# Moved steps in the attention queues, and compressed scores written 64 columns wide, in a hybrid SSD and sparse-attention block

## The chip, the cores and the metric

The kernel runs on one core of one Trainium2 chip. The metric is the device time of one execution in microseconds (us); less is better. A core has five queues that run side by side and meet only at semaphores: PE (TensorE, the matrix engine), DVE (VectorE), ACT (ScalarE), POOL (GpSimd) and SP (SyncE, which here issues the loads). Each queue works strictly in the order in which the kernel writes it down.

## The reference, cut to what matters

One layer takes a 512x1024 float32 input through a norm, a wide projection, a chunked state-space branch, an attention branch, a gated mix of both and an MLP. The change lies in the attention branch. It has 16 heads of 64 columns in 4 key groups, and three kinds of attention: over 31 compressed keys, over selected blocks and over a window. At 512 tokens the selection takes every block and the window covers every earlier token, so the last two are plain causal attention with different keys and values:

```python
s_c = jnp.einsum('bqgrd,bkgd->bgrqk', qn, kc).astype(jnp.float32) * scale
p_c = masked_softmax(s_c, cmp_end[None, :] <= t[:, None])
o_c = jnp.einsum('bgrqk,bkgd->bqgrd', p_c.astype(vc.dtype), vc)
...
s_s = jnp.einsum('bqgrd,bgqkd->bgrqk', qr, k_sel).astype(jnp.float32) * scale
p_s = masked_softmax(s_s, m_s)
o_s = jnp.einsum('bgrqk,bgqkd->bqgrd', p_s.astype(v_sel.dtype), v_sel)
...
o = gate[:, :, 0] * o_c + gate[:, :, 1] * o_s + gate[:, :, 2] * o_w
```

`qn` is the query before the rotary step, `qr` the one after it. `o_w` is made as `o_s`, with the window's keys and values.

## The kernel before, in words

The whole layer is one hand-scheduled program. Every large product is made in three parts to reach float32 accuracy: each operand is split into a high part (`whi`, `h_hi`, `q_hl`, `o_hi`) and the rest (`wlo`, `h_lo`, `o_lo`). A **unit** is one product of a 1024x128 block of weights with all 512 tokens: SP loads `raw`, ACT writes `whi` from it, POOL writes `wlo` (the function `low`, L834), PE multiplies. Two slots alternate.

Eight units make the queries (`q_unit`). After each, ACT writes a plain scaled copy `q_s` (`q_plain`), DVE makes the two products of the rotary step (`cos_q`), a small DMA swaps rows, DVE adds them (`rope_q`, L1520), ACT writes the high part (`high_q`) and DVE the low part (`low_q`, two halves of 64 rows, L1527). `cmp_scores(rr, pp)` multiplies `q_s` with the compressed keys `kc`: eight matmuls of 128 tokens each, whose results stand 64 columns apart in one bank. Seven of them are 128 columns wide, and the next one writes over the right half of what it left; only 64 columns of each are read, by `cmp_read` on DVE.

The attention itself is a loop over 64 **pairs** n. `pair(n)` gives the half of the heads rr (32 pairs each), the block of 128 tokens i (from 3 down to 0), the key group g, and br (0 selected, 1 window). A pair is two heads (r2), `width(n)` = 128 (i+1) keys wide: 512 for n 0 to 7, 384 for 8 to 15, then 256 and 128; the last two are `narrow`. The steps of a pair go round the engines:

- PE `scores(n)` (L2209, mask L2213), ahead of use by two pairs, or more for narrow ones (the table `ahead`)
- DVE `row_max(n)` (L1581, L1584; narrow L1578)
- ACT `exp(n, r2)` (L1005), which also sums the row
- DVE `over_sum(n)` (L1592), one over the sums
- POOL multiplies the probabilities with that and the gate (L854)
- PE `turn(n)` (L2248) transposes them, four 128x128 blocks a head at i=3, into one of two banks; before it takes a bank again it waits for the copy out of it two turns ago (`turn_to`, the list `copied`)
- ACT and DVE `copy_turned(n)` (L1041, L1606), one head each
- PE `weigh(n)` (L2269) multiplies with the values; for an odd n a matmul of the compressed part follows (L2277)
- ACT `high_out(a)` (L1012) and DVE `low_out(a)` (L1612) write the output of the two pairs 2a, 2a+1

The compressed part goes a block at a time: `cmp_centre`, `cmp_exp`, `cmp_probs`, `cmp_gates`, then PE `turn_cmp(c)` (L2236) and ACT `copy_cmp(c)` (L1022, writes `pcT`). `turn_cmp(0)` shares the two turn banks: it stands between the turns of pair 0 and pair 1, so it needs ACT's copy of pair 0, and the second head of `turn(1)` needs `copy_cmp(0)`.

The order around the change is written out by hand, one loop over n for each engine. Three things are in those loops that don't belong to the pairs: POOL's last two `low` (for the first two units of the state-space part, which PE reaches only after the attention), and the end of the query work for units 6 and 7, which the pairs from n=32 on use.

Of the kernel before, what the change touches and what calls it, by code (L numbers as in the profile page):

```python
# [28 lines left out]
P = 128  # L29
S = 512  # L30
# [35 lines left out]
U_SSM = U_Q + 8  # L66
# [69 lines left out]
def build(nc, a, out):  # L136

    ctx = ExitStack()
    with ctx:
# [364 lines left out]
        def narrow(n):  # L504
            return width(n) <= 256
# [319 lines left out]
        def _(pool):  # L825
# [18 lines left out]
            pool.wait_ge(whi_ready, U_SSM + 1)  # L844
            low(0)

            for n in range(PAIRS):
                rr, i, g, br = pair(n)
                pool.wait_ge(over_sum_ready, n + 1)
                for r2 in range(2):  # L850
                    at_step = 2 * n + r2
                    column = 16 * (br + 1) + g * R + 2 * rr + r2
                    rows = prob_rows(n, r2)
                    nc.gpsimd.tensor_scalar(rows, rows, rsum[:, at_step % 16:at_step % 16 + 1], gate[:, i, column:column + 1],  # L854
                                            ALU.mult, ALU.mult).then_inc(prob_ready, 1)
                if n == 2:
                    pool.wait_ge(whi_ready, U_SSM + 2)
                    low(1)
# [12 lines left out]
        def _(act):  # L871
# [181 lines left out]
            for n in range(PAIRS):  # L1053
                long = [m for m in ahead[n + 1] if not narrow(m)]
                if long:
                    exp(long[0], 0)
                if n == cmp_pair(0):
                    copy_cmp(0)
# [5 lines left out]
                for m in long[1:]:  # L1064
                    exp(m, 0)
                    exp(m, 1)
                for m in ahead[n + 1]:
                    if narrow(m):
                        exp(m, 0)
                        exp(m, 1)  # L1070
                if n % 8 == 2 and n < 58:
                    cmp_exp(n // 8 + 1)
                if n % 2 == 1 and n >= 3:
                    high_out((n - 3) // 2)
                if n in (2, 4):
                    high_q(5 + n // 2)
# [231 lines left out]
        def _(dve):  # L1308
# [213 lines left out]
            def low_q(u):  # L1522

                for e in range(2):
                    rows = slice(e * HD, (e + 1) * HD)
# [110 lines left out]
            low_q(5)  # L1636
            cos_q(7)
            for n in range(PAIRS):
                for m in ahead[n + 1]:
                    row_max(m)  # L1640
                for m in sums_at[n + 1]:
                    over_sum(m)
# [3 lines left out]
                if n < 2:  # L1646
                    rope_q(6 + n)
                if n == 2:
                    cmp_read(1, 1)
                if n in (3, 5):  # L1650
                    low_q(6 + n // 4)
# [381 lines left out]
        def _(pe):  # L2033
# [146 lines left out]
            def cmp_scores(rr, pp):  # L2180
# [7 lines left out]
                for i in range(NC):  # L2188
                    for r2 in range(2):
                        n = (i * 2 + r2) * 64  # L2190
                        w = min(P, S - n)
# [400 lines left out]
```

## Time and profile before

| | |
|---|---|
| median of 3 runs | 1281.34 us (1280.8 to 1281.37) |
| the profiled execution | 1279.05 us |
| its span in the trace | 1277.1 us |
| PE busy | 1247.4 us, 98% of the span |
| DVE, ACT, POOL busy | 763.3, 584.4, 404.0 us |
| granted TensorE clock | 0.998 of full speed |
| query units and attention | about 110 to 330 us |

The span is what lies between the first and the last instruction. A timeline row gives the start of a group of like instructions, how long they lasted together, the engine, the line, what is written and read, the shape, how many (xN), and in brackets the idle time of the engine before them and what ended it. A float32 matmul shows up as two records (two passes), each with its own weight load on the row PEld. Matmul records overlap each other, so a group's time holds the pipeline's depth once.

### The profile page before, as it was taken

The page shows a single profiled execution, that of the slowest core. Times are in us where ns is not written, and L with a number is a line of the kernel's source. Part 1 is how long each engine was busy: PE and PEld are TensorE (multiplying, and loading weights), DVE is VectorE, ACT ScalarE, POOL GpSimd, SP SyncE. Part 2 cuts the span into 40 slices and gives each one's busy share as a digit, 9 for nine tenths or more (in the row PEclk, how much of TensorE's full clock was granted, in tenths as well). Part 3 has the DMA queues.
Part 4 walks back from the last instruction along what each step waited for, and adds up shares of the span by engine and source line. Part 5 has one row for each costly group of instructions (what it writes and reads, how often), then busy time and mean ns, then how long its engine had stood idle before and what let it go on. Part 6 is the DMA issues. An engine that isn't in the chain of part 4 may idle for free.

```text
span 1277.1 us, 19195 instructions
## 1 busy us (share of the span) xinstructions
PE 1247.4 (98%) x6742; PEld 1026.5 (80%) x6742; DVE 763.3 (60%) x1353; ACT 584.4 (46%) x1016; POOL 404.0 (32%) x270
## 2 busy tenths in 40 slices
PE   8999989999999999999999999999999999999997
PEld 7887866777788888888888888888878888888885
DVE  6845876676477777877784111111147849479487
ACT  6325466666444544454453222222356446254364
POOL 3432344545332333333333444444430110201200
PEclk9999999999999999999999999999999999999999
DMA  8523410000123222322222333333443061340501
GB/s 242 157 70 71 93 37 2 2 2 2 50 66 83 68 80 66 82 66 72 76 70 79 98 91 93 97 99 108 172 161 119 17 214 33 112 151 16 201 12 66
DMA packets 172312, 108.40 MB, mean 85 GB/s; under 512 B 25220, under 2 KB 163814, under 8 KB 172262
## 3 DMA queue, kind: packets, MB, share of 16 engines
q1 hardware_dynamic: 172022, 107.65, 28.8%
q8 instruction: 30, 0.49, 0.2%
q14 instruction: 20, 0.16, 0.0%
q10 hardware_dynamic: 240, 0.09, 0.0%
HBM read 104.84 MB, written 2.10 MB: 84 GB/s over the span
## 4 chain that ended last, share of the span: by engine, by line
PE 86%; ACT 4%; DVE 4%; issue 2%; POOL 1%; DMA 1%; SPq 1%; DVEq 0%; ACTq 0%; POOLq 0%
PE bank L2424 20%; PE bank L2046 17%; PE bank L2433 10%; PE bank L2050 9%; PE bank L2528 8%; PE bank L2533 4%; PE bank L2443 2%; PE bank L2269 2%; PE bank L2209 2%; PE bank L2248 2%; ACT prob L1005 1%; POOL prob L854 1%; PE bank L2106 1%; PE bank L2449 1%; PE bank L2404 1%
## 5 line engine op out<-in xcount | busy, mean ns | idle before, releaser
L834 POOL TENSOR_TENSOR wlo<-raw,whi 128x1024 fp32r<-128x1024 f32 x133 | 325.1, 2445 | 717.7 <-ACT whi L1083 388.6
L1083 ACT ACTIVATE whi<-raw 128x1024 fp32r<-128x1024 f32 x96 | 101.8, 1060 | 295.7 <-PE bank L2433 160.0
L2046 PE MATMUL bank<-h_hi,whi 128*128 128x512 f32 x488 | 194.4, 398 | 0.7 <-DVE h_lo L1327 0.7
L2046 PE MATMUL bank<-h_lo,whi 128*128 128x512 f32 x488 | 190.4, 390 | 0.0
L2424 PE MATMUL bank<-h_hi,whi 128*128 128x512 f32 x384 | 150.3, 391 | 1.3 <-DVE grp L1766 0.7
L2424 PE MATMUL bank<-h_lo,whi 128*128 128x512 f32 x384 | 149.5, 389 | 0.0
L2050 PE MATMUL bank<-h_hi,wlo 128*128 128x512 f32 x488 | 120.8, 390 | 0.0
L2046 PEld LDWEIGHTS bank<-h_hi,whi 128*128 128x128 f32 x488 | 91.8, 188 | 21.1 <-DVE h_lo L1327 2.5
L1854 DVE TENSOR_TENSOR mt<-bank,sig 128x512 f32<-128x512 f32 x16 | 11.1, 691 | 161.6 <-PE bank L2433 161.6
L1746 DVE SCALAR_TENSOR_TENSOR grp<-bank,vt,grp 128x511 f32<-128x511 f32 (+2 forms) x96 | 71.8, 748 | 59.0 <-ACT grp L1107 50.1
L2050 PEld LDWEIGHTS bank<-h_hi,wlo 128*128 128x128 f32 x488 | 91.6, 188 | 19.1
L2046 PEld LDWEIGHTS bank<-h_lo,whi 128*128 128x128 f32 x488 | 91.8, 188 | 17.6
L854 POOL TENSOR_SCALAR prob<-prob,rsum,gate 128x512 f32<-128x512 f32 (+3 forms) x128 | 77.4, 619 | 79.2 <-DVE rsum L1592 79.1
L2433 PE MATMUL bank<-h_hi,wlo 128*128 128x512 f32 x384 | 94.8, 389 | 0.0
L2424 PEld LDWEIGHTS bank<-h_hi,whi 128*128 128x128 f32 x384 | 72.1, 188 | 18.5 <-DVE h_lo L1894 2.7
L1005 ACT ACTIVATE prob<-bank,nmax 128x512 f32<-128x512 f32 (+3 forms) x128 | 66.7, 531 | 44.0 <-DVE nmax L1581 38.5
L2433 PEld LDWEIGHTS bank<-h_hi,wlo 128*128 128x128 f32 x384 | 72.1, 188 | 15.0
L2424 PEld LDWEIGHTS bank<-h_lo,whi 128*128 128x128 f32 x384 | 72.1, 188 | 14.6
L1235 ACT ACTIVATE whi<-raw 128x1024 fp32r<-128x1024 f32 x30 | 31.7, 1057 | 79.2 <-PE bank L2433 60.9
L2248 PE MATMUL bank<-cst,prob 128*128 128x128 f32 x320 | 49.0, 278 | 12.6 <-POOL prob L854 9.5
L1917 DVE TENSOR_TENSOR comb<-comb 128x256 f32<-128x256 f32 x64 | 30.2, 492 | 49.5 <-ACT comb L1273 49.0
L1967 DVE TENSOR_TENSOR x<-bank,x 128x512 f32<-128x512 f32 x64 | 41.1, 683 | 21.3 <-PE bank L2533 21.3
(318 smaller groups left out, 2501.3 us busy)
## 6 DMA issues: line engine op xcount, KB each, us to landing
raw<-in_w_in SPq DMA_DIRECT2D x75, 512.0 KB, 3.8
raw<-in_w_up SPq DMA_DIRECT2D x32, 512.0 KB, 4.1
draw<-in_w_down SPq DMA_DIRECT2D x16, 1024.0 KB, 6.6
raw<-in_w_ssm_branch SPq DMA_DIRECT2D x16, 512.0 KB, 3.6
raw<-in_w_in SPq DMA_DIRECT2D x20, 256.0 KB, 3.8
raw<-in_w_attn_branch SPq DMA_DIRECT2D x8, 512.0 KB, 3.6
raw<-in_w_o SPq DMA_DIRECT2D x8, 512.0 KB, 3.7
x_sb<-in_x SPq DMA_DIRECT2D x4, 512.0 KB, 5.1
```

The source lines that it names most:

```text
L834: nc.gpsimd.tensor_tensor(wlo[slot][:], raw[slot][:], whi[slot][:].bitcast(F32), ALU.subtract).then_inc(wlo_ready, units)
L854: nc.gpsimd.tensor_scalar(rows, rows, rsum[:, at_step % 16:at_step % 16 + 1], gate[:, i, column:column + 1], ALU.mult, ALU.mult).then_inc( ...
L1005: nc.scalar.activation(prob_rows(n, r2), bank[b][:, off:off + width(n)], ACT.Exp, bias=nmax[:, at_step % 16:at_step % 16 + 1], accum_out=e ...
L1083: nc.scalar.activation(whi[slot][:], raw[slot][:], ACT.Copy).then_inc(whi_ready, 1)
L1746: ins = V.scalar_tensor_tensor(grp[:, j, back:S], bank[j % 2][:, 0:S - back], vt[:, bass.ds(tile + (V_CW + (CONV - 1 - back) * 32), 1)], g ...
L2046: T.matmul(bank[slot][:], whi[slot][:, k * P:(k + 1) * P], part[:, k, :], start=(k == 0 and n == 0), stop=False)
L2050: mm = T.matmul(bank[slot][:], wlo[slot][:, k * P:(k + 1) * P], h_hi[:, k, :], start=False, stop=(k == KT - 1))
L2248: mm = T.transpose(to[:, off + t * P:off + (t + 1) * P], prob_rows(n, r2)[:, t * P:(t + 1) * P], ident)
L2424: T.matmul(to[:], whi[slot][:, k * P:(k + 1) * P], part[:, k0 + k, :], start=(start and k == 0 and n == 0), stop=False)
L2433: mm = T.matmul(to[:], wlo[slot][:, k * P:(k + 1) * P], hi[:, k0 + k, :], start=False, stop=(stop and k == KT - 1))
L2528: T.matmul(bank[at_bank + t][:], part[:, 2 * (n % 2) + kl, which, t * P:(t + 1) * P], half_slot(n, 0)[:, kl, :], start=(fresh and n % 2 == ...
L2533: return T.matmul(bank[at_bank + t][:], comb_hi[:, 2 * (n % 2) + kl, which, t * P:(t + 1) * P], half_slot(n, 1)[:, kl, :], start=False, st ...
```

## The change

Six edits, all in the attention part:

1. POOL: the two `low` calls stood before the loop and after pair 2; now they stand after pair 1 and after pair 3.
2. ACT: at n=1 `copy_cmp(0)` goes ahead of the first exp of that round.
3. ACT: `high_out` goes ahead of the exps of narrow pairs. That moves it at n=13 and n=45 alone.
4. ACT and DVE: `high_q(7)` goes from n=4 to n=6, `rope_q(7)` from n=1 to n=4. `low_q(6)` went whole at n=3 and goes in halves at n=6 and 7; `low_q(7)` went whole at n=5 and goes in halves at n=8 and 10.
5. DVE: `over_sum(1)` goes from the loop's first round to a place ahead of `cos_q(7)`.
6. PE: all eight matmuls of `cmp_scores` are 64 columns wide.

```diff
--- before.py
+++ after.py
@@ -841,9 +841,6 @@
                 for slot in range(2):
                     pool.wait_ge(whi_ready, two * 2 + (slot + 1))
                     low(slot)
-            pool.wait_ge(whi_ready, U_SSM + 1)
-            low(0)
-
             for n in range(PAIRS):
                 rr, i, g, br = pair(n)
                 pool.wait_ge(over_sum_ready, n + 1)
@@ -853,9 +850,9 @@
                     rows = prob_rows(n, r2)
                     nc.gpsimd.tensor_scalar(rows, rows, rsum[:, at_step % 16:at_step % 16 + 1], gate[:, i, column:column + 1],
                                             ALU.mult, ALU.mult).then_inc(prob_ready, 1)
-                if n == 2:
-                    pool.wait_ge(whi_ready, U_SSM + 2)
-                    low(1)
+                if n in (1, 3):
+                    pool.wait_ge(whi_ready, U_SSM + n // 2 + 1)
+                    low(n // 2)
 
             with pool.Fori(U_SSM // 2 + 1, U_MLP // 2) as two:
                 for slot in range(2):
@@ -1052,10 +1049,10 @@
             q_split(7)
             for n in range(PAIRS):
                 long = [m for m in ahead[n + 1] if not narrow(m)]
+                if n == cmp_pair(0):
+                    copy_cmp(0)
                 if long:
                     exp(long[0], 0)
-                if n == cmp_pair(0):
-                    copy_cmp(0)
                 copy_turned(n)
                 if n and n % 8 == 0:
                     copy_cmp(n // 8)
@@ -1064,16 +1061,16 @@
                 for m in long[1:]:
                     exp(m, 0)
                     exp(m, 1)
+                if n % 2 == 1 and n >= 3:
+                    high_out((n - 3) // 2)
                 for m in ahead[n + 1]:
                     if narrow(m):
                         exp(m, 0)
                         exp(m, 1)
                 if n % 8 == 2 and n < 58:
                     cmp_exp(n // 8 + 1)
-                if n % 2 == 1 and n >= 3:
-                    high_out((n - 3) // 2)
-                if n in (2, 4):
-                    high_q(5 + n // 2)
+                if n in (2, 6):
+                    high_q(6 + n // 4)
             high_out(PAIRS // 2 - 1)
 
             def split_next(landed, done, slot):
@@ -1519,9 +1516,11 @@
                 roped = vtmp[:, u % 2, :]
                 V.tensor_tensor(roped, roped, rope_to[u % 2][:], ALU.add).then_inc(q_ready, 1)
 
-            def low_q(u):
+            def low_q(u, only=None):
 
                 for e in range(2):
+                    if only not in (None, e):
+                        continue
                     rows = slice(e * HD, (e + 1) * HD)
                     dve.wait_ge(qhi_ready, 2 * u + e + 1)
                     V.tensor_tensor(q_hl[(1 - e) * HD:(2 - e) * HD, 2 * u + e, :], vtmp[rows, u % 2, :],
@@ -1634,21 +1633,23 @@
             cmp_gates(0)
             cmp_read(1, 0)
             low_q(5)
+            over_sum(1)
             cos_q(7)
             for n in range(PAIRS):
                 for m in ahead[n + 1]:
                     row_max(m)
                 for m in sums_at[n + 1]:
-                    over_sum(m)
+                    if m >= 2:
+                        over_sum(m)
                 copy_turned(n)
                 if n % 2 == 1 and n >= 3:
                     low_out((n - 3) // 2)
-                if n < 2:
-                    rope_q(6 + n)
+                if n in (0, 4):
+                    rope_q(6 + n // 4)
                 if n == 2:
                     cmp_read(1, 1)
-                if n in (3, 5):
-                    low_q(6 + n // 4)
+                if n in (6, 7, 8, 10):
+                    low_q(6 + n // 8, (0, 1, 0, 1)[(6, 7, 8, 10).index(n)])
                 if n % 8 == 1 and n < 57:
                     cmp_centre(n // 8 + 1)
                 if n % 8 == 3 and n < 59:
@@ -2188,7 +2189,7 @@
                 for i in range(NC):
                     for r2 in range(2):
                         n = (i * 2 + r2) * 64
-                        w = min(P, S - n)
+                        w = 64
                         mm = T.matmul(to[:, n:n + w], q_s[:, 2 * pp + r2, i * P:(i + 1) * P],
                                       kc[:, pp, 0:w], start=True, stop=True)
                 mm.then_inc(cs_ready, 1)
```

Nothing is added and nothing taken out; SP's queue is as it was. Below are three places where it moves instructions. Line numbers of the changed kernel are up to three lower (L854 becomes L851, L1005 L1002, L1012 L1009, L1527 L1526).

**POOL, from the end of the loop over query units into the pairs.** `prob0` and `prob1` hold pair 0, `prob2` and `prob3` pair 1, `prob4` and `prob5` pair 2. Before:

```order
L834 TENSOR_TENSOR wlo0_68<-raw0_64,whi0_66 128x1024
L854 ISA
L854 TENSOR_SCALAR prob0_115<-prob0_115,rsum_110,gate_57 128x512
L854 TENSOR_SCALAR prob1_116<-prob1_116,rsum_110,gate_57 128x512
L854 TENSOR_SCALAR prob2_117<-prob2_117,rsum_110,gate_57 128x512
L854 TENSOR_SCALAR prob3_118<-prob3_118,rsum_110,gate_57 128x512
L854 TENSOR_SCALAR prob4_112<-prob4_112,rsum_110,gate_57 128x512
L854 TENSOR_SCALAR prob5_122<-prob5_122,rsum_110,gate_57 128x512
L834 TENSOR_TENSOR wlo1_69<-raw1_65,whi1_67 128x1024
L854 TENSOR_SCALAR prob0_115<-prob0_115,rsum_110,gate_57 128x512
```

Now:

```order
L851 TENSOR_SCALAR prob0_115<-prob0_115,rsum_110,gate_57 128x512
L851 TENSOR_SCALAR prob1_116<-prob1_116,rsum_110,gate_57 128x512
L851 TENSOR_SCALAR prob2_117<-prob2_117,rsum_110,gate_57 128x512
L851 TENSOR_SCALAR prob3_118<-prob3_118,rsum_110,gate_57 128x512
L834 TENSOR_TENSOR wlo0_68<-raw0_64,whi0_66 128x1024
L851 TENSOR_SCALAR prob4_112<-prob4_112,rsum_110,gate_57 128x512
L851 TENSOR_SCALAR prob5_122<-prob5_122,rsum_110,gate_57 128x512
L851 TENSOR_SCALAR prob0_115<-prob0_115,rsum_110,gate_57 128x512
L851 TENSOR_SCALAR prob1_116<-prob1_116,rsum_110,gate_57 128x512
L834 TENSOR_TENSOR wlo1_69<-raw1_65,whi1_67 128x1024
```

Both `wlo` rows moved down: the first from ahead of pair 0 to behind pair 1, the second from behind pair 2 to behind pair 3.

**ACT, in the round n=13.** `prob1` is the second head of pair 15, the rows with x2 are pairs 16 and 17, `o_hi` is `high_out(5)`, the `pT0` row behind is the copy of pair 14. Before:

```order
L1041 ACTIVATE pT0_128<-bank5 128x384
L1005 ACTIVATE prob1_116,esum_109<-bank1,nmax_108 128x384
L1005 ACTIVATE prob2_117,esum_109<-bank2,nmax_108 128x256 x2
L1005 ACTIVATE prob3_118,esum_109<-bank3,nmax_108 128x256 x2
L1012 ACTIVATE o_hi_72<-bank7 128x128
L1041 ACTIVATE pT0_128<-bank5 128x384
```

Now:

```order
L1038 ACTIVATE pT0_128<-bank5 128x384
L1002 ACTIVATE prob1_116,esum_109<-bank1,nmax_108 128x384
L1009 ACTIVATE o_hi_72<-bank7 128x128
L1002 ACTIVATE prob2_117,esum_109<-bank2,nmax_108 128x256 x2
L1002 ACTIVATE prob3_118,esum_109<-bank3,nmax_108 128x256 x2
L1038 ACTIVATE pT0_128<-bank5 128x384
```

`high_out(5)` moved up past the four exps of two narrow pairs. The same happens at n=45.

**DVE, in the rounds n=3 and n=4.** The first `pT0` row is the copy of pair 3, `o_lo` is `low_out(0)`, the three rows on `cst8` and `cs` are `cmp_probs(1)`, and `nmax` from bank2 and bank3 is `row_max(6)`. Before:

```order
L1592 RECIPROCAL rsum_110<-esum_109 128x2
L1606 COPY pT0_128<-bank4 128x512
L1612 TENSOR_TENSOR o_lo_73<-bank6,o_hi_72 128x128
L1527 TENSOR_TENSOR q_hl_119<-vtmp_96,q_hl_119 64x512 x2
L1555 TENSOR_REDUCE cst8_111<-cs_121 128x8
L1557 TENSOR_TENSOR cs_121<-cs_121,cst_49 128x2x128
L1559 RECIPROCAL cst8_111<-cst8_111 128x8
L1581 TENSOR_REDUCE nmax_108<-bank2 128x1
L1584 TENSOR_REDUCE nmax_108<-bank3 128x1
```

Now:

```order
L1591 RECIPROCAL rsum_110<-esum_109 128x2
L1605 COPY pT0_128<-bank4 128x512
L1611 TENSOR_TENSOR o_lo_73<-bank6,o_hi_72 128x128
L1554 TENSOR_REDUCE cst8_111<-cs_121 128x8
L1556 TENSOR_TENSOR cs_121<-cs_121,cst_49 128x2x128
L1558 RECIPROCAL cst8_111<-cst8_111 128x8
L1580 TENSOR_REDUCE nmax_108<-bank2 128x1
L1583 TENSOR_REDUCE nmax_108<-bank3 128x1
```

The two halves of `low_q(6)` are gone from between `low_out(0)` and `row_max(6)`. The same holds for `low_q(7)` two rounds on.

## Rows read from the trace of the kernel before

**Rows 1.** The page: PE's busy time (share of the span), and the chain by engine.

```profile
PE 1247.4 (98%) x6742; PEld 1026.5 (80%) x6742; DVE 763.3 (60%) x1353; ACT 584.4 (46%) x1016; POOL 404.0 (32%) x270
...
PE 86%; ACT 4%; DVE 4%; issue 2%; POOL 1%; DMA 1%; SPq 1%; DVEq 0%; ACTq 0%; POOLq 0%
```

**Rows 2.** Waits of PE over the whole span: total, times, longest in us.

```profile
PE bank L2248 <- POOL prob L854: 9.5, 8, 3.0
...
PE bank L2248 <- ACT pcT L1022: 1.4, 1, 1.4
```

**Rows 3.** Timeline of PE, 163 to 196 us: start, duration, work, [idle before].

```profile
166.35 1.41 PE L2248 MATMUL bank<-cst,prob 128*128 128x128 f32 x8 [2.96 <-POOL prob L854]
...
167.51 0.70 PE L2209 MATMUL bank<-kw,q_hl 128*128 128x512 f32 x2
...
168.71 0.39 PE L2236 MATMUL bank<-cst,cs 128*128 128x128 f32 x2
...
170.93 0.63 PE L2248 MATMUL bank<-cst,prob 128*128 128x128 f32 x4 [1.39 <-ACT pcT L1022]
...
173.75 1.04 PE L2248 MATMUL bank<-cst,prob 128*128 128x128 f32 x8
...
186.76 1.41 PE L2248 MATMUL bank<-cst,prob 128*128 128x128 f32 x8 [0.92 <-POOL prob L854]
...
194.77 1.41 PE L2248 MATMUL bank<-cst,prob 128*128 128x128 f32 x8 [1.27 <-POOL prob L854]
```

**Rows 4.** Timeline of POOL, 162 to 175 us.

```profile
162.80 2.67 POOL L834 TENSOR_TENSOR wlo<-raw,whi 128x1024 fp32r<-128x1024 f32 x1 [11.76 <-ACT whi L977]
165.53 3.03 POOL L854 TENSOR_SCALAR prob<-prob,rsum,gate 128x512 f32<-128x512 f32 x4
...
171.95 2.38 POOL L834 TENSOR_TENSOR wlo<-raw,whi 128x1024 fp32r<-128x1024 f32 x1
```

**Rows 5.** Timeline of ACT, 165 to 171 us.

```profile
165.19 0.69 ACT L1005 ACTIVATE prob<-bank,nmax 128x512 f32<-128x512 f32 x1 [1.05 <-DVE nmax L1581]
...
167.04 0.60 ACT L1041 ACTIVATE pT<-bank 128x512 f32<-128x512 f32 x1 [1.07 <-PE bank L2248]
...
170.41 0.37 ACT L1022 ACTIVATE pcT<-bank 128x256 f32<-128x256 f32 x1
```

**Rows 6.** Timeline of DVE, 155 to 184 us.

```profile
155.71 0.17 DVE L1592 RECIPROCAL rsum<-esum 128x2 f32<-128x2 f32 x1 [0.70 <-ACT prob L1005]
...
172.20 2.67 DVE L1520 TENSOR_TENSOR vtmp<-vtmp,rope_to 128x512 f32<-128x512 f32 x1
...
182.18 1.40 DVE L1527 TENSOR_TENSOR q_hl<-vtmp,q_hl 64x512 fp32r<-64x512 f32 x2
```

**Rows 7.** Timeline of PE, turns of pairs 13 and 15, 213 to 221 us.

```profile
213.35 0.82 PE L2248 MATMUL bank<-cst,prob 128*128 128x128 f32 x6
...
219.87 1.20 PE L2248 MATMUL bank<-cst,prob 128*128 128x128 f32 x6 [1.62 <-POOL prob L854]
```

**Rows 8.** Timeline of PE, turn of pair 47, 298 us.

```profile
298.49 1.19 PE L2248 MATMUL bank<-cst,prob 128*128 128x128 f32 x6 [1.63 <-POOL prob L854]
```

**Rows 9.** Timeline of ACT, round n=13, 214 to 217 us.

```profile
214.82 0.48 ACT L1005 ACTIVATE prob<-bank,nmax 128x256 f32<-128x256 f32 x1
...
216.62 0.31 ACT L1012 ACTIVATE o_hi<-bank 128x128 fp32r<-128x128 f32 x1
```

**Rows 10.** Timeline of DVE, `low_out(5)` in round n=13.

```profile
216.96 0.29 DVE L1612 TENSOR_TENSOR o_lo<-bank,o_hi 128x128 fp32r<-128x128 f32 x1 [2.19 <-ACT o_hi L1012]
```

**Rows 11.** Timeline of PEld, wide passes of the first `cmp_scores`.

```profile
127.37 0.75 PEld L2192 LDWEIGHTS bank<-kc,q_s 128*128 128x128 f32 x6
```

**Rows 12.** Timeline of PEld, last two wide and both 64-column passes, next unit's load.

```profile
128.27 0.53 PEld L2192 LDWEIGHTS bank<-kc,q_s 128*128 128x128 f32 x4
128.71 0.19 PEld L2175 LDWEIGHTS bank<-h_hi,whi 128*128 128x128 f32 x1
```

**Rows 13.** Timeline of PE, eight 512-column matmuls of a query unit.

```profile
151.86 1.98 PE L2175 MATMUL bank<-h_hi,wlo 128*128 128x512 f32 x8
```

## The prediction

> **What bounds the kernel now.** The page comes first: PE is busy 98% of the span, and 86% of the chain that ended last is PE's [rows 1]. So time is won only where PE stands still or does less. The waits of PE come second: its one large item is `turn` waiting for POOL's multiplied probabilities, 9.5 us in 8 places, and one of 1.4 us for ACT's `pcT` [rows 2]. The timeline of PE comes third, to see where these lie: 2.96 us before `turn(0)`, 1.39 before the second head of `turn(1)`, 0.92 before `turn(5)`, 1.27 before `turn(7)` [rows 3], 1.62 before `turn(15)` [rows 7], and 1.63 at the same place of the second half, `turn(47)` [rows 8]. They sum to 9.8 us. The reader should see that each has another releaser behind the one named: POOL is a relay, and what made it late is found on POOL, ACT and DVE.
>
> A turn that had to wait also runs slower, since its second head's probabilities come while the first is being turned: 1.41 us for eight records against 1.04 for one that never waited [rows 3], 1.20 for six against 0.82 [rows 7], 1.19 for pair 47 [rows 8]. That is 0.37 us more at each of the last four places. At `turn(0)` I count nothing more, since POOL was then working through both pairs anyway.
>
> **The change part by part.**
>
> *POOL's first `low`, and `over_sum(1)`.* The sums of pair 0 were inverted on DVE at 155.71 [rows 6], but POOL first did `wlo` from 162.80 to 165.47 and only then pair 0 at 165.53 [rows 4]. Now pair 0 is ready before PE wants it: the 2.96 us go. What is late next is ACT. PE's wait began at 166.35 - 2.96 = 163.39. From there it does `turn(0)` in about 1.0 us and `scores(3)` in 1.2 (167.51 to 168.71), and at about 165.6 comes to `turn_cmp(0)`, which needs ACT's copy of pair 0. ACT does that behind the first exp of pair 2, begun at 165.19 [rows 5]; with `over_sum(1)` now ahead on DVE I take 165.3. Exp 0.69 and copy 0.60 give 166.6: a new wait of 1.0 us.
>
> *`copy_cmp(0)` ahead of an exp.* Before, `pcT` was written at 170.41, behind an exp [rows 5] whose row maximum came late; PE got on at 170.93. Now it stands right behind the second exp of pair 2: 166.6 + 0.69 + 0.37 = 167.6, while PE, with 0.2 for `turn_cmp` and 0.44 for four transposes, is there at 167.3. The wait of 1.39 becomes 0.3. Left of both: 1.3 us. `over_sum(1)` itself is 0.17 us on DVE and gives POOL pair 1 early, so that `wlo` (2.4 us) fits in ahead of pair 2.
>
> *Where `wlo` now falls.* `rope_q(7)` took 2.67 us when it ran beside the second `wlo`, ending 0.5 us after it [rows 4, 6]; its like take 0.7. Now `rope_q(6)` falls beside the first `wlo` (about 165.0 to 167.4) and should end near 167.9. Pair 2 is then multiplied from about 169.1, its first head done at 169.9; PE turns it at about 170.4. Hidden, with half a microsecond in hand. The two `wlo` blocks themselves end at most 2 us later than before. The loads of SP that wait for them, and PE's use of them, belong to the part behind the attention, some 150 us on: nothing.
>
> *`low_q` out of rounds 3 and 5.* `low_q(6)` held DVE for 1.40 us at 182.18 [rows 6], ahead of `row_max(6)` and `over_sum(5)`, and `turn(5)` waited 0.92 for that; `low_q(7)` did the same to `turn(7)`, 1.27. Taking 1.4 us out of the way is more than either. Gone: 0.92 + 0.37 and 1.27 + 0.37, 2.9 us. The work comes back: 0.7 us of `rope_q(7)` in round 4, 0.7 in each of rounds 6, 7, 8 and 10, and 1.3 on ACT in round 6. Walking the queues with the durations of their rows, I find probabilities ready some 0.4 us before PE wants them in rounds 7 to 13, so a bare 0.7 us mostly fits. But in even rounds the piece stands right behind `over_sum`, when POOL starts on two multiplications of 0.76 us each (3.03 for four [rows 4]), and it reads two tiles of SBUF as `rope_q(7)` did. Waiting one of them out is 0.76, or 0.36 over the margin; for three such pieces about 0.9 us is paid back (bounds: 0, and three times 0.76, 2.3).
>
> By the Trainium skill (SBUF — State Buffer, "Who interferes with whom") a tensor_tensor with both inputs in SBUF contends with GpSimd's reads, and whichever starts first blocks the other for its whole instruction. The 2.67 us beside `wlo` agree. By that rule every piece beside a multiplication pays, and the payback is nearer its upper bound.
>
> *`high_out` ahead of narrow exps.* In round 13 ACT went through four exps of pairs 16 and 17, from 214.82 to 216.62, before `high_out(5)` [rows 9]. DVE stood 2.19 us for it [rows 10], and behind `low_out(5)` lay `over_sum(15)`, for which `turn(15)` waited. DVE gets on 1.8 us sooner; the wait was 1.62. Gone: 1.62 + 0.38, and 1.63 + 0.37 at `turn(47)`, 4.0 us. The exps start 0.3 us later; DVE inverts their sums only behind two more row maxima.
>
> *64 columns in place of 128.* 28 matmuls, 56 passes. Six weight loads of wide passes start within 0.75 - 0.19 = 0.56 us, 0.112 apart [rows 11]. The last four, two of them for 64-column passes, start within 0.53 - 0.19 = 0.34, 0.113 apart, and the next unit's load follows at 128.71, no sooner [rows 12]. A narrow pass takes as long as a wide one, because its 128 columns of weights do. Bounds: 0, and 3.1 us (56 times half of 0.112) if the pass shrank with its columns. I take 0, the row that is the thing itself.
>
> By the Trainium skill (TensorE: Matmul & The Clock Gate, "Step-by-step: what each phase is for") a matmul's throughput is purely its N moving columns. By that rule 64 columns fewer at 2.4 GHz would save an estimated 27 ns a pass, 1.5 us in all. In this trace a 512-column matmul costs 0.227 us, (1.98 - 0.39) / 7 [rows 13], so streaming does set the pace there, at 0.44 ns a column.
>
> **The sum.** Removed: 2.96 + 1.39 + 1.29 + 1.64 + 2.00 + 2.00 = 11.3 us. Left at the start 1.3, paid back 0.9. Gain 9.1 us. From the profiled execution's 1279.05 that is 1269.9; from the median, which lies 2.3 higher, 1281.34 - 9.1 = **1272.2 us**.
>
> **The rivals.**
>
> *The ring of DVE and ACT takes over.* DVE waits for `o_hi`, ACT for the row maximum, so one round feeds the next. With PE's early stalls gone, the 2.8 us of DVE work moved into rounds 6 to 10 comes where the margin is thin, and the waits at `turn(5)`, `turn(7)` and `turn(15)` come back at other turns. For: DVE had the same work in all. Against: its 2.19 us of idle time in round 13. It keeps 11.3 - 1.3 - 4.9 = 5.1 us: 1276.2.
>
> *The narrow writes count.* The forecast less 1.6 us (56 passes by 64 columns by 0.44 ns [rows 13]) to 3.1: 1270.6 to 1269.1. Against: the loads' pace [rows 12].
>
> *Waits only move.* `turn_cmp(0)` stands as long as `turn(0)` did, ACT being slower through `high_q(5)` and the last splits than I think, and the later stalls shift. About 1280.
>
> *Slower.* Place: rounds 6 to 10. Price: four halves of `low_q` at 0.7, each waiting 0.76 for POOL, and `high_q(7)` at 1.3 ahead of an exp: 7.1 us on a ring that is then the bound, with only `turn(47)`'s 2.0 kept: 1286.4. It decides once DVE has no idle time left in rounds 8 to 13. The 2.19 us [rows 10] speak against it.
>
> **How the numbers follow.** Forecast 0.62 (its own range 1270.3 to 1274.5), ring 0.20, narrow writes 0.08, waits only move 0.06, slower 0.04. A difference of 0.2%, 2.6 us, is about what a measurement can tell from none. Three cases are faster by more: 0.90; same 0.06, slower 0.04. The range takes in the first three, 1269.0 to 1277.0.
>
> **What would show it.** The waits of PE for POOL fall from 9.5 us to under 3. `turn(15)` and `turn(47)` wait for nothing, and DVE's 2.19 us before `o_lo` are gone. In round 1 a wait of about 1 us for ACT's copy stands before `turn_cmp(0)`. Weight loads of `cmp_scores` are still 0.112 us apart. It is wrong if new waits of PE for POOL stand in rounds 7 to 13 (then the ring), if the loads come closer together (then the narrow writes), or if PE waits some 3 us before `turn_cmp(0)`.

## The result: 1271.6 us, and the profile after

The changed kernel takes **1271.59 us** (median of 4 runs, 1270.12 to 1272.79), the kernel before 1281.07 beside it (4 runs). The ratio is 0.9927, 95% interval 0.991 to 0.9944: 7.2 to 11.5 us less. 1272.2 was forecast.

The page of the changed kernel, answering to [rows 1]:

```profile
PE 1249.4 (98%) x6742; PEld 1030.6 (81%) x6742; DVE 762.2 (60%) x1353; ACT 583.8 (46%) x1016; POOL 405.3 (32%) x270
...
PE 87%; DVE 4%; ACT 3%; issue 2%; POOL 1%; DMA 1%; SPq 1%; DVEq 0%; ACTq 0%; POOLq 0%
```

PE is as busy as before in a shorter span, and still carries the chain. The waits of PE (line waited for: total, times, longest), answering to [rows 2]:

```profile
PE bank L2249 <- POOL prob L851: 1.4, 4, 0.4
...
PE bank L2237 <- ACT pT L1038: 1.3, 1, 1.3
```

For POOL it waits 1.4 us in place of 9.5, and no wait for `pcT` is long enough to be listed. New is one of 1.3 before `turn_cmp(0)` (L2237). PE's timeline has the places of [rows 3, 7, 8]; `turn` is now L2249:

```profile
168.43 0.41 PE L2237 MATMUL bank<-cst,cs 128*128 128x128 f32 x2 [1.32 <-ACT pT L1038]
168.69 1.34 PE L2249 MATMUL bank<-cst,prob 128*128 128x128 f32 x8
...
202.95 0.55 PE L2249 MATMUL bank<-cst,prob 128*128 128x128 f32 x3 [0.27 <-POOL prob L851]
...
214.20 1.20 PE L2249 MATMUL bank<-cst,prob 128*128 128x128 f32 x6
...
291.18 1.19 PE L2249 MATMUL bank<-cst,prob 128*128 128x128 f32 x6
```

In order these are `turn_cmp(0)`, `turn(1)`, the second head of `turn(11)`, `turn(15)` and `turn(47)`. The last two have no wait that is listed (PE is idle 0.03 us before each), but take 1.20 and 1.19 us, as long as before.

**The start.** ACT and POOL at the same place, answering to [rows 4, 5]:

```profile
167.02 0.69 ACT L1002 ACTIVATE prob<-bank,nmax 128x512 f32<-128x512 f32 x1 [1.11 <-DVE nmax L1580]
...
167.70 0.59 ACT L1038 ACTIVATE pT<-bank 128x512 f32<-128x512 f32 x1
...
168.87 0.38 ACT L1019 ACTIVATE pcT<-bank 128x256 f32<-128x256 f32 x1
```

```profile
165.30 1.52 POOL L851 TENSOR_SCALAR prob<-prob,rsum,gate 128x512 f32<-128x512 f32 x2 [6.04 <-DVE rsum L1591]
166.78 2.35 POOL L834 TENSOR_TENSOR wlo<-raw,whi 128x1024 fp32r<-128x1024 f32 x1
```

POOL now does pair 0 first. ACT copies pair 0 behind the exp that began at 167.02, and `turn_cmp(0)` follows that copy. The copy of `pcT` ends at 169.25, while PE is in `turn(1)`, and the second head of that turn starts right behind it:

```profile
169.40 0.30 PE L2249 MATMUL bank<-cst,prob 128*128 128x128 f32 x1
```

That is late as well: the turn takes 1.34 us for eight records, 1.04 where nothing is late. It is too short a gap (0.08 us of idle time) to be listed as a wait.

**Rounds 4 to 13.** DVE, with `rope_q(6)` and `rope_q(7)` (L1517), the four halves of `low_q` (L1526) and `low_out(5)` (L1611), answering to [rows 6, 10]:

```profile
168.10 1.58 DVE L1517 TENSOR_TENSOR vtmp<-vtmp,rope_to 128x512 f32<-128x512 f32 x1
...
183.17 0.90 DVE L1517 TENSOR_TENSOR vtmp<-vtmp,rope_to 128x512 f32<-128x512 f32 x1
...
189.32 0.79 DVE L1526 TENSOR_TENSOR q_hl<-vtmp,q_hl 64x512 fp32r<-64x512 f32 x1
...
193.35 0.69 DVE L1526 TENSOR_TENSOR q_hl<-vtmp,q_hl 64x512 fp32r<-64x512 f32 x1
...
195.65 0.81 DVE L1526 TENSOR_TENSOR q_hl<-vtmp,q_hl 64x512 fp32r<-64x512 f32 x1
...
201.54 0.81 DVE L1526 TENSOR_TENSOR q_hl<-vtmp,q_hl 64x512 fp32r<-64x512 f32 x1
...
211.06 0.29 DVE L1611 TENSOR_TENSOR o_lo<-bank,o_hi 128x128 fp32r<-128x128 f32 x1 [0.36 <-ACT o_hi L1009]
```

The wait before `low_out(5)` is 0.36 us; it was 2.19. POOL's multiplications in these rounds:

```profile
185.48 1.53 POOL L851 TENSOR_SCALAR prob<-prob,rsum,gate 128x512 f32<-128x512 f32 x2 [0.76 <-DVE rsum L1591]
188.81 1.95 POOL L851 TENSOR_SCALAR prob<-prob,rsum,gate 128x512 f32<-128x512 f32 x2 [1.80 <-DVE rsum L1591]
191.56 1.30 POOL L851 TENSOR_SCALAR prob<-prob,rsum,gate 128x384 f32<-128x384 f32 x2 [0.81 <-DVE rsum L1591]
195.26 1.73 POOL L851 TENSOR_SCALAR prob<-prob,rsum,gate 128x384 f32<-128x384 f32 x2 [2.39 <-DVE rsum L1591]
...
201.16 1.74 POOL L851 TENSOR_SCALAR prob<-prob,rsum,gate 128x384 f32<-128x384 f32 x2 [2.08 <-DVE rsum L1591]
```

A pair that a piece of `low_q` fell beside took 1.95 us in place of 1.53, or 1.73 in place of 1.30. The piece beside it took 0.79 to 0.81, and 0.69 where it fell beside none (193.35). The two heads of the pair at 188.81, one by one:

```profile
188.81 0.77 POOL L851 TENSOR_SCALAR prob<-prob,rsum,gate 128x512 f32<-128x512 f32 x1 [1.80 <-DVE rsum L1591]
...
189.55 1.20 POOL L851 TENSOR_SCALAR prob<-prob,rsum,gate 128x512 f32<-128x512 f32 x1
```

The first took its usual 0.77; the piece (189.32 to 190.11) began only 0.25 us before that ended; the second took 1.20, so all of POOL's 0.43 lies there.

**Where the 9.1 us lie.** From the first query unit's first matmul to the last matmul of the attention, the changed kernel takes 207.75 us, the kernel before 216.84: 9.09 us less. I call this the **stretch** from here on. Behind it the two traces keep their distance. The profiled executions themselves lie only 6.3 us apart (1272.79 and 1279.05): this one lost 1.7 us ahead of the stretch, where the program is the same, and 1.0 us more of its time lies outside the trace's span (1272.79 less 1269.8, against 1279.05 less 1277.1). The first 17 us of the changed kernel, then of the one before (busy time, PE's with records, granted clock, DMA share, GB/s):

```profile
0.00:17.00 17.00, 14.09 (x85) 0.90 0.81 231
```

```profile
0.00:17.00 17.00, 13.71 (x90) 1.00 0.84 233
```

The clock there was 0.90 against 1.00. So I compare stretches. Each is that of one execution.

The sum can be checked inside the stretch: for each pair, its turn's start is counted from the first query unit's matmul in both traces, and the difference is what has been gained so far.

| up to | forecast, this part | measured, this part | gained so far |
|---|---|---|---|
| turn(3) | 3.05 (4.35 removed, 1.3 left) | 2.99 | 2.99 |
| turn(6) | 1.29 | 1.44 | 4.43 |
| turn(8) | 1.64 | 1.79 | 6.22 |
| turn(14) | -0.9 | -0.42 | 5.80 |
| turn(15) | 2.00 | 1.59 | 7.39 |
| turn(47) | 2.00 | 1.60, and 0.05 between | 9.04 |

### The profile page after: what moved, and what is told of

Same layout as the page of the kernel before. It is cut to its first block, busy times and chain, and to the rows that moved or that the text cites. A ratio compares the mean times of both kernels' runs of the same rounds, so it can differ in the third digit from the quotient of the medians.

```text
span 1269.8 us, 19195 instructions
## 1 busy us (share of the span) xinstructions
PE 1249.4 (98%) x6742; PEld 1030.6 (81%) x6742; DVE 762.2 (60%) x1353; ACT 583.8 (46%) x1016; POOL 405.3 (32%) x270
## 4 chain that ended last, share of the span: by engine, by line
PE 87%; DVE 4%; ACT 3%; issue 2%; POOL 1%; DMA 1%; SPq 1%; DVEq 0%; ACTq 0%; POOLq 0%
PE bank L2425 21%; PE bank L2047 17%; PE bank L2434 10%; PE bank L2051 8%; PE bank L2529 8%; PE bank L2534 4%; PE bank L2270 2%; PE bank L2444 2%; PE bank L2210 2%; PE bank L2249 2%; POOL prob L851 1%; PE bank L2107 1%; PE bank L2450 1%; PE bank L2405 1%; ACT prob L1002 1%
## 5 line engine op out<-in xcount | busy, mean ns | idle before, releaser
L851 POOL TENSOR_SCALAR prob<-prob,rsum,gate 128x512 f32<-128x512 f32 (+3 forms) x128 | 78.9, 629 | 80.7 <-DVE rsum L1591 80.7
L1002 ACT ACTIVATE prob<-bank,nmax 128x512 f32<-128x512 f32 (+3 forms) x128 | 66.7, 534 | 37.0 <-DVE nmax L1580 33.8
L2249 PE MATMUL bank<-cst,prob 128*128 128x128 f32 x320 | 48.6, 278 | 2.9 <-POOL prob L851 1.4
```

What stands on the lines that cost most here:

```text
L1002: nc.scalar.activation(prob_rows(n, r2), bank[b][:, off:off + width(n)], ACT.Exp, bias=nmax[:, at_step % 16:at_step % 16 + 1], accum_out=e ...
L2249: mm = T.transpose(to[:, off + t * P:off + (t + 1) * P], prob_rows(n, r2)[:, t * P:(t + 1) * P], ident)
```

## The experiments

The theory: the gain comes from PE's six waits, each ended by work moved out of an engine's queue; the narrow writes do nothing. Its rivals: the narrow writes carry part of it; or edits only pay in company. Four kernels are the kernel before with one part of the change alone. (Edits 2 and 5 were not run alone.) Each ratio below is to the kernel before as timed in the same session (medians 1280.02, 1281.16 and 1280.81 us), with its 95% interval; it can differ from the quotient of the medians by 0.1%.

**Narrow writes alone.**

```diff
-                        w = min(P, S - n)
+                        w = 64
```

> The kernel before, with the 64-column writes alone. The attention stretch (first query-unit matmul to the last attention matmul) was 216.84 us before and 207.75 with the whole change. Theory (a pass is paced by the load of its 128 weight columns): the loads stay 0.112 us apart, the stretch stays at 216.8 within 0.1, the time within 0.1% of before. Rival (a pass costs its moving columns): 56 passes shorter by 0.028 to 0.056, so the stretch is 215.3 to 213.7.

Measured: 1280.77 us, ratio 1.0007 (0.9997 to 1.0017), stretch 216.91 against 216.84. `turn(0)`, behind three of the four blocks, starts 0.01 us earlier than before. They are worth nothing.

**`high_out` alone.**

```diff
+                if n % 2 == 1 and n >= 3:
+                    high_out((n - 3) // 2)
                 for m in ahead[n + 1]:
                     if narrow(m):
```

> The kernel before, with high_out ahead of the narrow exps alone. Theory (ACT's four exps of 1.8 us stand before high_out(5), DVE's low_out(5) and the sums of pair 15): the waits of 1.62 and 1.63 before turn(15) and turn(47) go to 0.1, the second head of each turn still comes late, the stretch is 216.84 - 3.2 = 213.6, the time 3.2 us less. Rival (POOL, or the row maxima of pairs 18 and 19 ahead of the sums, hold turn(15)): waits of 1 us and more stay, gain under 1.5.

Measured: 1276.02 us, ratio 0.9967 (0.9954 to 0.9979), stretch 213.87: 2.97 less. Counted up to each turn, 1.59 come at `turn(15)` and 1.6 at `turn(47)`; 0.17 was lost at the start, on which more below.

**POOL's `low` and `over_sum(1)` alone.**

```diff
-            pool.wait_ge(whi_ready, U_SSM + 1)
-            low(0)
...
-                if n == 2:
+                if n in (1, 3):
...
+            over_sum(1)
             cos_q(7)
```

> The kernel before, with POOL's low and over_sum(1) moved alone. Theory (the wait of 2.96 is replaced by one for ACT's copy, and pcT is still behind an exp whose row maximum is late): PE waits about 1.3 before turn_cmp(0) and about 1.1 for pcT, gain 1.5 to 2.0 of the 4.35 that both first waits cost. Rival (the whole 2.96 goes, since pair 0 is all that PE lacked): gain 3 or more.

Measured: 1281.01 us, ratio 1.0008 (0.9998 to 1.0017), and the stretch 1.4 us **longer**, 218.28. That is a miss. PE's timeline of this kernel:

```profile
166.62 0.41 PE L2235 MATMUL bank<-cst,cs 128*128 128x128 f32 x2 [1.40 <-ACT pT L1038]
166.86 0.60 PE L2247 MATMUL bank<-cst,prob 128*128 128x128 f32 x4
169.71 1.08 PE L2247 MATMUL bank<-cst,prob 128*128 128x128 f32 x4 [2.24 <-ACT pcT L1019]
170.72 1.98 PE L2268 MATMUL bank<-pT,vtok 128*64 128x128 f32 x16
172.63 1.22 PE L2208 MATMUL bank<-ks,q_hl 128*128 128x512 f32 x2
```

The 2.96 us are gone, but 1.40 and 2.24 took their place, and what follows is slow: `weigh` (L2268) took 1.98 us for sixteen records that take 1.09 elsewhere. The granted clock says why:

```profile
168.00:170.00 2.00, 0.29 (x2) 0.76 0.61 164
170.00:172.00 2.00, 2.00 (x16) 0.50 0.36 107
...
174.00:176.00 2.00, 2.00 (x9) 0.53 0.00 0
```

From about 169.0, in the second wait, to 175.9 PE's clock was at 0.50, its level of 1.2 GHz. The wait of 2.24 is for `pcT`, which ACT writes behind an exp whose row maximum stands on DVE behind `rope_q(6)`, itself slowed by `wlo`:

```profile
166.28 1.59 DVE L1517 TENSOR_TENSOR vtmp<-vtmp,rope_to 128x512 f32<-128x512 f32 x1
167.80 0.68 DVE L1578 TENSOR_REDUCE nmax<-bank 128x1 f32<-128x512 f32 x1
```

```profile
168.51 0.69 ACT L1002 ACTIVATE prob<-bank,nmax 128x512 f32<-128x512 f32 x1 [1.37 <-DVE nmax L1578]
...
169.19 0.37 ACT L1019 ACTIVATE pcT<-bank 128x256 f32<-128x256 f32 x1
```

**The same, with `copy_cmp(0)` ahead of that exp.**

```diff
+                if n == cmp_pair(0):
+                    copy_cmp(0)
                 if long:
                     exp(long[0], 0)
-                if n == cmp_pair(0):
-                    copy_cmp(0)
```

> The kernel before, with POOL's low and over_sum(1) moved and copy_cmp(0) ahead of the exp. In the run of the POOL edit alone PE waited 1.40 and then 2.24 us, the granted clock fell to 0.50 from about 169.5 to 175.8 us, and the stretch grew to 218.3. Theory (the exp in front of pcT makes the second wait, and the two waits together bring the clock down): with copy_cmp(0) moved too PE waits 1.3 and at most 0.3, the clock stays at 1.00, the stretch is 216.84 - 3.0 = 213.8. Rival (POOL's order alone brings the clock down or shifts the stall): clock at 0.50 again, stretch over 215.5.

Measured: 1276.93 us, ratio 0.9969 (0.996 to 0.9978), stretch 213.69. The waits are 1.30 before `turn_cmp(0)` and 0.24 for POOL in `turn(2)`; the clock is 1.00 throughout. The two edits are worth 3.15 us of the stretch together, and without the second the first costs 1.4.

**Is the clock the difference?** The kernel of POOL's `low` and `over_sum(1)` again, with matmuls that nobody reads put where PE waits: five ahead of `turn_cmp(0)`, nine ahead of the second head of `turn(1)`.

```diff
+            def filler(count):
+                pe.wait_ge(q_cos_ready, 7)
+                for _ in range(count):
+                    T.matmul(bank[6][:, 2 * P:3 * P], ones[:], ones[:], start=True, stop=True)
```

> The kernel with POOL's low and over_sum(1) moved alone, with 5 matmuls of ones that nobody reads before turn_cmp(0) and 9 before the second head of turn(1), so that PE works through most of its waits of 1.40 and 2.24 us. Theory (that kernel's loss of 1.4 us comes from the granted clock at 0.50 after the waits): the clock stays at 1.00, and the stretch falls from 218.3 to about 216.1, less than the 216.84 of before. Rival (the loss is the longer wait for pcT and what follows it on the queues): it stays at 218 or more.

Measured: 1278.66 us, ratio 0.9983 (0.9973 to 0.9992), stretch 215.35. Two rows of its PE timeline, and the clock:

```profile
167.34 2.17 PE L2230 MATMUL bank<-ones 128*128 128x128 f32 x18
...
170.31 1.09 PE L2277 MATMUL bank<-pT,vtok 128*64 128x128 f32 x16
```

```profile
170.00:172.00 2.00, 2.00 (x24) 1.00 0.42 125
...
174.00:176.00 2.00, 2.00 (x24) 1.00 0.00 0
```

`turn(1)`'s second head came no sooner (169.72 against 169.71), yet `weigh` takes 1.09 us again and the stretch is 2.9 us shorter. So the drop cost 2.9 us, and without it the POOL edit alone gains 1.5, as first expected. The loss isn't that of one execution: over ten each the medians differ by 2.35 us (1281.01 and 1278.66).

**`low_q`, `rope_q` and `high_q` alone.** The diff is edit 4 of the change.

> The kernel before, with high_q, rope_q and low_q of units 6 and 7 moved alone. Theory: the waits before turn(5) and turn(7) go, 0.92 + 1.27 us and 0.3 to 0.7 of late second heads, and rope_q(7) no longer stands 2.67 us beside the second wlo, with nothing gained at the start: gain 2.5 to 3. Rival (the moved work is paid back in rounds 6 to 13): gain under 1.5, with new waits before turns 8 to 13.

Measured: 1277.77 us, ratio 0.9984 (0.9974 to 0.9993), stretch 215.77, only 1.07 less. By turns it had gained 1.25 at `turn(6)`, 3.03 at `turn(8)` and 2.61 from `turn(12)` to `turn(47)`, as expected; then it lost 1.5. PE's clock around `turn(47)`:

```profile
290.00:296.00 6.00, 4.38 (x46) 1.00 0.00 0
...
298.00:300.00 2.00, 2.00 (x11) 0.50 0.00 0
300.00:302.00 2.00, 2.00 (x15) 0.71 0.00 0
```

PE stood still for 1.62 us in the first of these, as at [rows 8], and this time the clock fell to 0.50 behind it. In the profile of before it didn't. Whether the other nine executions of this kernel had this drop isn't shown: by the medians it gains 2.25 us (1280.02 less 1277.77), more than its stretch does.

**The change without that edit.** The same three functions put back in the changed kernel:

```diff
-                if n in (2, 6):
-                    high_q(6 + n // 4)
+                if n in (2, 4):
+                    high_q(5 + n // 2)
...
-                if n in (0, 4):
-                    rope_q(6 + n // 4)
+                if n < 2:
+                    rope_q(6 + n)
...
-                if n in (6, 7, 8, 10):
-                    low_q(6 + n // 8, (0, 1, 0, 1)[(6, 7, 8, 10).index(n)])
+                if n in (3, 5):
+                    low_q(6 + n // 4)
```

> The changed kernel with high_q, rope_q and low_q of units 6 and 7 back in their old rounds. Theory: waits of about 1 us each before turn(5) and turn(7) are back, the stretch is 207.75 + 2.5 = 210.2. Rival (with the rest of the change in, DVE has slack and they cost nothing): 208.

Measured: 1273.12 us, ratio to before 0.9948 (0.9931 to 0.9965), stretch 210.65. The waits are back at `turn(5)` (0.59) and `turn(7)` (1.25). The edit is worth 2.9 us in company. The parts now add up: 3.15 (start) + 2.97 (`high_out`) + 2.90 + 0 (narrow writes) = 9.02, against 9.09 for the whole.

**What a narrow pass costs.** Two kernels make every compressed-score matmul six times over, one 64 and one 128 columns wide; the repeats write the same numbers.

```diff
-                        w = 64
+                        w = min(P, S - n)
-                        mm = T.matmul(to[:, n:n + w], q_s[:, 2 * pp + r2, i * P:(i + 1) * P],
-                                      kc[:, pp, 0:w], start=True, stop=True)
+                        for _ in range(6):
+                            mm = T.matmul(to[:, n:n + w], q_s[:, 2 * pp + r2, i * P:(i + 1) * P],
+                                          kc[:, pp, 0:w], start=True, stop=True)
```

> The changed kernel with every compressed-score matmul issued six times, 64 columns wide: 320 more passes of 64 columns. Theory (a pass is paced by its weight load, 0.112 us): the four blocks last about 10.7 us each in place of 1.8, the stretch grows by at most 36 us, and as much as in the 128-column twin. Rival (columns set the pace): half of that, 18 us.

> The same with 128 columns (seven of eight matmuls, as before the change). Theory: the same length as the 64-column twin within 0.5 us. Rival: 18 us longer than the twin.

Measured, one execution each: 1306.63 us with 64 columns, 1306.54 with 128; stretches 242.91 and 242.62. Counted from the first query unit's matmul, every turn of the two up to pair 16 starts at the same time to 0.01 us; the 0.3 comes later, with a wait of 0.38 for POOL (264.12) that the wide one doesn't have. The matmuls' own durations (least, median, most ns), 64 columns first:

```profile
L2194 PE MATMUL bank<-kc,q_s x384: 217/275/275, 128.2 to 210.9; 128*128 128x64 f32 x192
```

```profile
L2194 PE MATMUL bank<-kc,q_s x384: 222/275/328, 128.8 to 211.5; 128*128 128x128 f32 x168, 128*128 128x64 f32 x24
```

320 passes more cost 35.2 us in the narrow form and 34.9 in the wide one, 0.11 us each either way: the 0.112 us between weight loads of [rows 11, 12]. By the Trainium skill (TensorE: Matmul & The Clock Gate, "LDWEIGHTS (loading the stationary operand)") a load takes the number of its columns over 1.2 in ns, an estimated 107 for 128 columns. These runs agree within 5%.

**Can the new 1.3 us wait go?** In the changed kernel ACT copies pair 0 ahead of its exps of round 0, and does `copy_cmp(0)` between them.

```diff
-                if n == cmp_pair(0):
+                if n == 0:
+                    copy_turned(0)
+                    exp(2, 0)
                     copy_cmp(0)
+                    exp(2, 1)
+                    continue
```

> The changed kernel, with ACT's copy of pair 0 ahead of the first exp of pair 2 and copy_cmp(0) ahead of the second. Theory (the wait of 1.32 us before turn_cmp(0) is ACT's order alone): it goes to under 0.2, the stretch is 207.75 - 1.2 = 206.5. Rival (DVE is the one that is late, with rope_q(6) 1.58 us beside wlo): the wait moves to a later turn and the stretch stays over 207.3.

Measured: 1270.2 us, ratio to before 0.9921 (0.9906 to 0.9937), stretch 207.90, no shorter. The wait changed hands:

```profile
166.45 1.06 PE L2253 MATMUL bank<-cst,prob 128*128 128x128 f32 x8 [0.95 <-DVE pT L1609]
...
170.04 0.66 PE L2253 MATMUL bank<-cst,prob 128*128 128x128 f32 x4 [0.17 <-POOL prob L851]
171.03 0.66 PE L2253 MATMUL bank<-cst,prob 128*128 128x128 f32 x4 [0.33 <-POOL prob L851]
```

```profile
165.03 0.68 DVE L1587 TENSOR_REDUCE nmax<-bank 128x1 f32<-128x512 f32 x1
165.62 0.68 DVE L1609 COPY pT<-bank 128x512 f32<-128x512 f32 x1
166.22 1.62 DVE L1521 TENSOR_TENSOR vtmp<-vtmp,rope_to 128x512 f32<-128x512 f32 x1
```

Now DVE's copy of the other head (L1609) is late, behind both row maxima of pair 2, and `rope_q(6)` beside `wlo` delays the sums of pair 2, for which `turn(2)` waits twice.

**More of the same.** On top of that, sums ahead of row maxima on DVE where all pairs ahead are narrow, and the halves of `low_q` in odd rounds, behind `low_out`.

```diff
+                sums_first = all(narrow(m) for m in ahead[n + 1])
+                if not sums_first:
+                    for m in ahead[n + 1]:
+                        row_max(m)
                 for m in sums_at[n + 1]:
...
-                if n in (6, 7, 8, 10):
+                if n in (7, 9, 11, 13):
```

> The changed kernel with three more moves: ACT's copies early as in the run before, the halves of low_q in the odd rounds 7, 9, 11 and 13 behind low_out, and the sums ahead of the row maxima where all pairs ahead are narrow. Theory: 1.2 us for the first, 0.3 for the second (the wait of 0.27 before the second head of turn(11)), 0.37 each for turn(15) and turn(47), and 1.1 for the waits of 0.38, 0.34 and 0.37 in the narrow pairs: stretch 204.4, time 3.3 us under the changed kernel. Rival (the narrow waits have another cause than the order of sums and maxima): stretch 205.5 or more.

Measured: 1268.69 us, ratio 0.9908 (0.9894 to 0.9921), stretch 206.04. Half of what was expected. The sums gained 1.2 by pair 28, 0.2 of it at `turn(15)`, and 1.3 more in the second half; by `turn(14)` it stood 0.8 behind the changed kernel, 0.2 of that from the start and 0.6 from the odd rounds, where a new wait of 0.37 stands before `turn(11)` (202.17).

**The best version.** The changed kernel with sums first, `low_q` as in the change, and a start in which both copies of pair 0 and `copy_cmp(0)` go ahead, `rope_q(6)` at n=2 and `high_q(6)` at n=4.

```diff
-                if n == cmp_pair(0):
+                if n == 0:
+                    copy_turned(0)
                     copy_cmp(0)
+                    exp(2, 0)
+                    exp(2, 1)
+                    continue
...
+                if n == 0:
+                    copy_turned(n)
...
-                if n in (0, 4):
-                    rope_q(6 + n // 4)
+                if n in (2, 4):
+                    rope_q(5 + n // 2)
```

> The changed kernel with the sums ahead of the row maxima where all pairs ahead are narrow, and a new start: ACT does the copy of pair 0 and copy_cmp(0) ahead of both exps of pair 2, DVE does its copy of pair 0 ahead of row_max(2), rope_q(6) goes to round 2, behind the first wlo, and high_q(6) to round 4; low_q stays as in the changed kernel. Theory: at the start the wait of 1.32 before turn_cmp(0) goes and none takes its place, 1.2 us; sums first gave 1.2 us by pair 28 and 1.3 more by pair 60 in the run of all three moves, 2.4: stretch 204.2, time 3.5 us under the changed kernel. Rival (the exps of pair 2, now 0.6 us later, hold turn(2)): stretch 205.2.

Measured: **1267.11 us** (1266.03 to 1267.7), ratio to before 0.9886 (0.987 to 0.9903), stretch 203.57. What PE still waits for in the attention:

```profile
PE bank L2261 <- POOL prob L851: 0.5, 2, 0.3
```

`turn_cmp(0)` waits for nothing, and 4.2 us of the stretch are gone beside the changed kernel.

## Why the prediction was right

All six waits are gone or under 0.1 us, by the ways named, and the sum, 9.08, met 9.09 in the stretch. That it met so closely is luck: its parts were off by 0.1 to 0.75 us, and they cancel.

One thing is common to all the waits and the prediction left it out: a wait costs about 0.16 us more than the idle time listed for it. In the changed kernel `turn(3)` starts 0.07 us behind the start of the matmul ahead of it, inside that one's record (177.65, 0.23 us long). In the kernel before the same matmul ahead of `turn(5)` starts at 185.60 and the turn at 186.76, 1.16 behind: 1.09 later than without a wait, for 0.92 of idle time.

- **Start, 4.35 removed, 1.3 left: 2.99 of 3.05.** The net was met, its parts weren't. Removed were 5.04: the two waits, 0.16 more for each, and 0.37 of a slow `turn(0)` (1.41 us before, 1.04 now), which the prediction put at nothing. Left are 2.05: the wait before `turn_cmp(0)`, put at 1.0, is 1.32 for the copy named, and costs 1.48; the 0.3 for `pcT` came, as the late second head of `turn(1)`; and `turn(2)`, which was called hidden with half a microsecond in hand, has a late second head too (1.31 us for 1.04). POOL's multiplication for it took 1.01 us in place of 0.77. What I missed is that the two edits are no separate terms. I priced the `pcT` wait as one that edit 2 takes away; the run without edit 2 shows that edit 1 by itself makes it longer, 2.24.
- **`low_q` out of rounds 3 and 5: 1.44 and 1.79 for 1.29 and 1.64.** The waits and the 0.37 of the late second head both went. The 0.15 more in each is what a wait costs beyond its idle time, 1.09 for the 0.92 before `turn(5)`.
- **Payback: 0.42 for 0.9.** The step that failed is "waiting one of them out is 0.76". The piece doesn't start with POOL's first multiplication but half a microsecond behind it (189.32 and 188.81), since DVE copies a turned head first. So only 0.25 is left to wait out, and DVE's piece takes 0.1 more; the bill goes to POOL, whose second multiplication takes 0.43 more. (And three times 0.36 is 1.1, not the 0.9 of the sum.) So three pieces cost POOL 0.43 each, nearly all of it inside the margin, and only the last, at 201.16, came through, as the 0.27 before `turn(11)`'s second head at 202.95 and its slower turn.
- **`high_out`: 1.6 at each place for 2.00.** The wait went down to 0.03, but the 0.37 for the late second head stayed. I counted it as caused by the wait. It is caused by the distance between POOL's two heads, 0.64 us, where both still come only just in time: 1.20 us for six records with no wait listed. At `turn(5)` and `turn(7)` it went, because there POOL is well ahead. "Sums first" brings POOL ahead here as well: in the best version `turn(15)` and `turn(47)` take 0.82 us.
- **Narrow writes: 0 of 0.** Read rightly from the pace of the loads. The rule set against it, that throughput is purely the moving columns, would have given 1.5 us, and six times that in the pair of kernels with repeats; the narrow one of these is no shorter, but 0.3 longer.
- **The rivals.** The ring of DVE and ACT didn't take over: DVE's idle time in round 13 fell to 0.36 us but didn't vanish, and `turn(15)` waited 0.03. The "slower" case priced four pieces at 0.76 of waiting each; the three that met a multiplication paid 0.1 each.

Not foreseen at all: the clock. No step of the prediction has it, since the profile of before shows 1.00 behind the 2.96 us.

## What to carry to other kernels

Follow a wait through the engine named as its releaser (a relay here) to the first one that did something else, and price edits at one junction together: here the first alone cost 1.4 us and with the second gained 3.15. Count the slow turn behind a wait as gained only if the second head's input will be there in time as well. Before pricing a collision of two engines, read from the rows how much of the first instruction is left when the second starts. Writing 64 columns in place of 128 saved nothing here, where every pass loads 128 columns of new weights.

## What the hardware did that I had not expected

**The clock behind short waits.** The granted clock fell to 0.50 for some 3 to 7 us when PE had stood still for 3.0 us (three of the kernels with the old start: 0.50 at 168 to 170 with the narrow writes alone and with `high_out` alone, 0.51 with `low_q` alone), for 1.40 and most of 2.24 close together, and once for 1.62; eleven other waits of 1.62 or 1.63 in these profiles had no drop behind them. It didn't in the profiled execution of before, with the same waits. In the kernels whose longest wait at the start was 1.41 us or less it stayed at 1.00 there. Behind the 3.0 us the drop was nearly free (at most 0.2 in the end), since the wait for `pcT` that came next shrank by as much, from 1.39 to 0.21 or less; with no such wait behind it, it cost 2.9 us and 1.5. So a wait can cost more than its length, and not in every execution. How long PE must stand for it is open.

**Who pays at a collision of DVE and POOL.** Beside `wlo` a DVE addition of 0.7 us took 1.58 to 2.67 and `wlo` its usual 2.4. Beside the multiplications DVE paid 0.1 to 0.2 and POOL 0.43. By the Trainium skill (SBUF — State Buffer, "Who interferes with whom") who starts first blocks the other for its instruction. The rows agree, with some 0.15 us off. Before, `rope_q(7)` started with 2.12 us of `wlo` to go and took 1.98 more than its 0.69; in the changed kernel `rope_q(6)` had 1.03 to go and took 0.89 more. `rope_q(7)` there had 0.36 of a multiplication to go and took 0.20 more, the three pieces of `low_q` 0.25 to 0.28 and 0.10 to 0.12 more. POOL's next multiplication then started 0.56 us before DVE's instruction ended, and took 0.43 more, in all four cases. So what is paid follows how much of the other's instruction is left. The kernel before had a case of this size too: at 168.40 `rope_q(6)` started with 0.16 us of a multiplication to go and took 0.70 us, next to nothing more.
